# A hybrid decoder layer on one core: weight differences issued earlier, and seven products in place of eight in part of the last gate projection

## The reference, cut to what matters

```
hn = rms_norm(h, ffn_norm)
h  = h + (silu(hn @ w_gate) * (hn @ w_up)) @ w_down          # 2048 -> 5632 -> 2048
gate = sigmoid(rms_norm(h, ple_norm) @ w_ple_gate)           # 2048 -> 2048, "the last gate projection"
h  = h + gate * (p @ w_ple_proj)                             # 256 -> 2048
```

## Time and profile before

| what | value |
|---|---|
| median of three runs | 1309.48 us |
| the profiled execution's own time | 1309.3 us |
| its span, first to last instruction | 1307.6 us |
| TensorE busy | 1300.2 us, 99% of the span |
| VectorE busy | 1025.2 us, 78% |
| ScalarE busy | 705.4 us, 54% |
| mean granted TensorE clock | 0.999 |

### The profile page before, as it was taken

One profiled execution on the slowest core, in us unless ns is written; L12 is line 12 of the kernel. 1 busy time (PEld: TensorE's weight loads), 2 busy tenths in 40 slices (PEclk: granted clock), 3 DMA queues, 4 the chain that ended last, 5 costly groups with the idle time before them and its releaser, 6 DMA issues.

```text
span 1307.6 us, 18471 instructions
## 1 busy us (share of the span) xinstructions
PE 1300.2 (99%) x6595; PEld 1073.5 (82%) x6595; DVE 1025.2 (78%) x1381; ACT 705.4 (54%) x937; POOL 56.6 (4%) x71
## 2 busy tenths in 40 slices
PE   9999999999999999999999999999999999999998
PEld 7788888887888887888888888888888888888887
DVE  6578885788586668999988987679888997968554
ACT  6576444543455566655555654445555555555643
POOL 5003000221000000000000000000000000000000
PEclk9999999999999999999999999999999999999999
DMA  8555544455434555665566656565566556556563
GB/s 272 177 177 162 161 146 130 146 149 152 145 119 145 184 170 165 218 213 186 183 208 205 198 189 210 186 212 187 191 206 209 191 178 210 194 178 207 193 201 138
DMA packets 126205, 238.38 MB, mean 182 GB/s; under 512 B 9711, under 2 KB 10786, under 8 KB 126138
## 3 DMA queue, kind: packets, MB, share of 16 engines
q1 hardware_dynamic: 126106, 237.48, 56.9%
q10 hardware_dynamic: 32, 0.01, 0.0%
HBM read 235.36 MB, written 2.10 MB: 182 GB/s over the span
## 4 chain that ended last, share of the span: by engine, by line
PE 97%; DVE 2%; ACT 0%; issue 0%; POOL 0%; DVEq 0%; ACTq 0%; POOLq 0%
PE pair L635 16%; PE pair L637 16%; PE pair L636 16%; PE pair L916 11%; PE pair L917 11%; PE pair L918 11%; PE bg L916 2%; PE bg L917 2%; PE bg L918 2%; PE bg L756 2%; PE bg L826 2%; PE bg L911 1%; PE bg L693 1%; DVE w_lo L1504 1%; PE bg L807 0%; PE bg L668 0%
## 5 line engine op out<-in xcount | busy, mean ns | idle before, releaser
L1504 DVE TENSOR_TENSOR w_lo<-raw,w_hi 128x1024 fp32r<-128x1024 f32 x442 | 533.4, 1222 | 180.9 <-ACT w_hi L1107 179.0
L1107 ACT ACTIVATE w_hi<-raw 128x1024 fp32r<-128x1024 f32 x401 | 419.3, 1056 | 274.9 <-PE pair L637 148.6
L635 PE MATMUL pair<-w_hi,xT_hi 128*128 128x512 f32 x780 | 314.3, 403 | 0.3 <-DVE w_lo L1763 0.2
L637 PE MATMUL pair<-w_hi,xT_lo 128*128 128x512 f32 x780 | 304.8, 391 | 0.0
L636 PE MATMUL pair<-w_lo,xT_hi 128*128 128x512 f32 x780 | 304.2, 390 | 0.0
L637 PEld LDWEIGHTS pair<-w_hi,xT_lo 128*128 128x128 f32 x780 | 146.4, 188 | 31.5
L635 PEld LDWEIGHTS pair<-w_hi,xT_hi 128*128 128x128 f32 x780 | 146.5, 188 | 29.9 <-issue 0.9
L636 PEld LDWEIGHTS pair<-w_lo,xT_hi 128*128 128x128 f32 x780 | 146.8, 188 | 27.3
L1379 ACT ACTIVATE w_hi<-raw 128x1024 fp32r<-128x1024 f32 x41 | 43.6, 1063 | 134.6 <-DVE raw L1830 133.1
L916 PE MATMUL pair<-w_hi,actT_hi 128*128 128x512 f32 x296 | 115.9, 392 | 0.0
L918 PE MATMUL pair<-w_hi,actT_lo 128*128 128x512 f32 x296 | 115.3, 389 | 0.0
(11 more groups left out here) (351 smaller groups left out, 1882.8 us busy)
## 6 DMA issues: line engine op xcount, KB each, us to landing
raw<-in_w_in_dram SPq DMA_DIRECT2D x112, 512.0 KB, 3.7
raw<-in_w_gate_dram SPq DMA_DIRECT2D x88, 512.0 KB, 4.4
raw<-in_w_up_dram SPq DMA_DIRECT2D x88, 512.0 KB, 4.5
raw<-in_w_down_dram SPq DMA_DIRECT2D x88, 512.0 KB, 4.7
raw<-in_w_o_dram SPq DMA_DIRECT2D x32, 512.0 KB, 4.0
raw<-in_w_ple_gate_dram SPq DMA_DIRECT2D x32, 512.0 KB, 4.5
raw<-in_w_ple_proj_dram SPq DMA_DIRECT2D x4, 512.0 KB, 4.2
h<-in_x_dram SPq DMA_DIRECT2D x3, 512.0 KB, 8.1
```

Source lines behind the costliest of these rows:

```text
L635: mm(banks[t][:], hi[:, ts], wh, start=first, stop=False)
L637: m = mm(banks[t][:], lo[:, ts], wh, start=False, stop=last)
L1107: f(w_hi[j % RING][:], raw[j % RING][:], ACT.Copy).then_inc(hi_ready, 1)
L1504: v.tensor_tensor(w_lo[j % RING][:], raw[j % RING][:], w_hi[j % RING][:].bitcast(F32), ALU.subtract).then_inc(lo_ready, 1)
```

## The change

There are two edits.

1. **Differences of the first mixed pair.** The four DVE differences for F5 and F6 were issued in the turn of F3, just before the remainder of F6. Now they are issued in the turn of F1 (`EARLY = 1`), after the remainder of F4 and before the DVE part of step `hA` 6. Two small buffers of the `hA` steps move elsewhere, and the fetch of F9 now also waits for the remainder of F5.
2. **Seven products in the last gate projection.** Blocks 0 and 1 are computed together in 16 units (`PG_SEQ`): five units of block 0 (k pairs 0, 1, 2, 3, 7), then three mixed pairs (k pairs 4, 5, 6), each followed by one plain unit of block 1, and two more plain ones. So L5/L6, L8/L9 and L11/L12 are mixed. Blocks 2 and 3 stay as they were. `hB` 4, 5 and 6 now also make four differences of activations each; `hB` 4 stands in the turn of P1, `hB` 5 in that of P2, `hB` 6 and 7 still in that of P3. ACT copies P1 to P3 out ahead of these steps and no longer behind. The squares of the last block of `h` move from the end of the down projection to the turn of L1, the sum over them to the turn of L3. The sums of partial results come in the turn of L12 and of L15, and block 0 is finished in the turn of L13, block 1 in that of L17.

```diff
-            at[(U_DB + FF_B * 8 // KU + 3, U_DB + FF_B * 8 // KU + 5, U_PP - 2, U_PP + 3)[n]][g].append(("hB", 2 * n + g))
+            late = (U_PP + 1 + g, U_PP + 3)[n - 2] if n > 1 else 0
+            at[late or U_DB + FF_B * 8 // KU + 3 + 2 * n][g if n != 2 else 0].append(("hB", 2 * n + g))
+EARLY = 1
+PG_MIXED = (4, 5, 6)
+PG_PLAIN = [g for g in range(UPB) if g not in PG_MIXED]
+PG_SEQ = ([(0, g) for g in PG_PLAIN] + [(0, PG_MIXED[0]), (1, PG_MIXED[0]), (1, PG_PLAIN[0])]
+          + [(0, PG_MIXED[1]), (1, PG_MIXED[1]), (1, PG_PLAIN[1])]
+          + [(0, PG_MIXED[2]), (1, PG_MIXED[2])] + [(1, g) for g in PG_PLAIN[2:]])
# SyncE, first gate/up block
                             sp.wait_ge(t4_ready, ...)
+                            if seq is FIRST_SEQ:
+                                sp.wait_ge(lo_ready, u0 + j - (RING - 1))
# TensorE, a mixed pair of the last gate projection
+                    use(u)
+                    product(bg[0][:], xT_hi[:, k0, a0], xT_lo[:, k0, a0], gh[:, 0, :], gl[:, 0, :], first, last)
+                    product(pair[0][0][:], xT_hi[:, k1, a0], ..., gh[:, 1, :], gl[:, 1, :], False, last).then_inc(unit_used, 1)
+                    use(u + 1)
+                    product(bg[3][:], E_hi[:, q, 0, :], ..., uh[:, 0, :], ul[:, 0, :], first, last)
+                    product(pair[1][0][:], E_hi[:, q, 2, :], ..., uh[:, 1, :], ul[:, 1, :], first, False).then_inc(unit_used, 1)
+                    pe.wait_ge(t3_lo_ready, MIX_PG + q + 1)
+                    product(bg[2][:], E_hi[:, q, 3, :], ..., t_hi[:, 2, :], t_lo[:, 2, :], first, last)
+                    pe.wait_ge(t24_lo_ready, MIX_PG + q + 1)
+                    product(bg[1][:], E_hi[:, q, 1, :], ..., t_hi[:, 0, :], t_lo[:, 0, :], first, last)
+                    product(pair[0][1][:], xT_hi[:, k1, a1], ..., t_hi[:, 1, :], t_lo[:, 1, :], False, last).then_inc(t_used, 1)
# ACT, step hB 4, 5, 6 (after the two scaled copies into xg)
+                            f(xT_hi[:, 2 * b:2 * b + 2, :], xg[:], ACT.Copy).then_inc(x_hi, 2)
+                            act.wait_ge(form_ready, 4 * (c + 1))
+                            f(E_hi[:, q, :, :], F_raw[:], ACT.Copy).then_inc(form_rounded, 1)
# ACT, turns of P0 to L31
+                if side and g in PG_MIXED:
+                    split_mixed(u + LEAD, u + LEAD, MIX_PG + PG_MIXED.index(g) + 1, False)
+                elif u + LEAD < UNITS:
                     split(u + LEAD, u + LEAD)
+                if u < U_PG:
+                    pp_end(u - U_PP)
                 for k in range(2):
                     for s in AT[u][k]:
                         post(*s)
+                if u == U_PG + 1:
+                    res_squares(3)
+                if u == U_PG + PG_END:
+                    act.wait_ge(t_used, MIX_PG + len(PG_MIXED))
+                    f(act_s[1][:], bg[0][:], ACT.Copy).then_inc(p1_copied, 1)
+                    act.wait_ge(h_rstd, 4)
+                    for t in range(NT):
+                        act.wait_ge(gate_sum, 2 * (FF_A + FF_B) + t + 1)
+                        f(gate_s[t][:], gate_s[t][:], ACT.Sigmoid, scale=h_rs[1][:, t:t + 1]).then_inc(pair_free[0], 1)
# DVE
+            def split_mixed(u, j, n, first, between):
+                if not first:
+                    dve.wait_ge(lo_ready, u)
+                    differences(u, j, n)
                 split(u, j)
...
                         split(u, j + LEAD)
+                    if peeled and n0 == 0 and j == EARLY:
+                        differences(u0 + seq.index(("up", MIXED[0])), seq.index(("up", MIXED[0])), m0 + 1)
                     if peeled:
                         for k in range(2):
                             for s in AT[u0 + j][k]:
                                 post(*s)
...
+                if u == U_PG + 3:
+                    dve.wait_ge(h_sq, 16)
+                    v.reduce_sum(h_s[1][:], h_ss[1][:], AX_X).then_inc(h_sum, 1)
+                if u == U_PG + PG_END:
+                    dve.wait_ge(p1_copied, done + 4 + 1)
+                    v.tensor_tensor(v_s[:], bg[1][:], act_s[1][:], ALU.add).then_inc(v_ready, 1)
+                    ...            # five more sums of 128x512, two of them ready for the sigmoids
+                if u == U_PG + PG_END + 1:
+                    finish(0, gate_s, pair_free[0], 2 * (B_PG // 2))
+                if u == U_PG + 2 * UPB - 1:
+                    wait_block(dve, u)
+                    dve.wait_ge(pg_parts, 2)
+                    for t, part in ((0, v_s), (1, u_s)):
+                        v.tensor_tensor(act_s[t][:], pair[1][t][:], part[:], ALU.add).then_inc(pair_free[1], 1)
+                if u == U_PG + 2 * UPB + 1:
+                    finish(1, act_s, pg_sig, 0)
```

More of the change, by code:

```diff
@@ L283, in build @@
         t3_raw = sb("t3_raw", [P, CB], at=mix + 62 * KIB)
-        d_raw = sb("d_raw", [P, 2, P], at=mix + 62 * KIB)
-        h1_raw = sb("h1_raw", [P, 2, P], at=mix + 63 * KIB)
+        d_raw = sb("d_raw", [P, 2, P], at=mix + 52 * KIB)
+        h1_raw = sb("h1_raw", [P, 2, P], at=mix + 53 * KIB)
         xg = sb("xg", [P, 2, TOK], at=mix + 58 * KIB)
@@ L512, in _ @@
                 load(U_PP + b, b, w_pp, 0, b * CB)
-            with sp.Fori(0, 2) as i:
-                for j in range(2 * UPB):
-                    load(i * (2 * UPB) + (U_PG + j), j, w_pg, KU * (j % UPB), i * (2 * CB) + j // UPB * CB)
+            for j, (side, g) in enumerate(PG_SEQ):
+                if j >= RING and PG_SEQ[j - RING] in [(0, m) for m in PG_MIXED]:
+                    sp.wait_ge(t4_ready, MIX_PG + PG_MIXED.index(PG_SEQ[j - RING][1]) + 1)
+                    fetch(j, w_pg, KU * g, side * CB)
+                else:
+                    load(U_PG + j, j, w_pg, KU * g, side * CB)
+            for j in range(2 * UPB, 4 * UPB):
+                load(U_PG + j, j, w_pg, KU * (j % UPB), j // UPB * CB)
             for b in range(3):
@@ new lines, in _ @@
+            a0, a1 = slice(0, P), slice(P, TOK)
+            pe.wait_ge(pair_free[0], 2 * (B_PG // 2))
+            for j, (side, g) in enumerate(PG_SEQ):
+                u = U_PG + j
+                k0, k1 = KU * g, KU * g + 1
+                if not side:
+                    wait_read(pe, ("hB", g))
+                if g in PG_MIXED:
+                    if side:
+                        continue
+                    q = PG_MIXED.index(g)
+                    first, last = q == 0, q == len(PG_MIXED) - 1
+                    if first:
+                        pe.wait_ge(pair_free[1], 2 * ((B_PG + 1) // 2))
+                        for n in PG_MIXED:
+                            wait_read(pe, ("hB", n))
+                    gh, gl = w_hi[j % RING], w_lo[j % RING]
+                    uh, ul = w_hi[(j + 1) % RING], w_lo[(j + 1) % RING]
+                    use(u)
+                    product(bg[0][:], xT_hi[:, k0, a0], xT_lo[:, k0, a0], gh[:, 0, :], gl[:, 0, :], first, last)
+                    product(pair[0][0][:], xT_hi[:, k1, a0], xT_lo[:, k1, a0], gh[:, 1, :], gl[:, 1, :], False,
+                            last).then_inc(unit_used, 1)
+                    use(u + 1)
+                    product(bg[3][:], E_hi[:, q, 0, :], E_lo[:, q, 0, :], uh[:, 0, :], ul[:, 0, :], first, last)
+                    product(pair[1][0][:], E_hi[:, q, 2, :], E_lo[:, q, 2, :], uh[:, 1, :], ul[:, 1, :], first,
+                            False).then_inc(unit_used, 1)
+                    pe.wait_ge(t3_lo_ready, MIX_PG + q + 1)
+                    product(bg[2][:], E_hi[:, q, 3, :], E_lo[:, q, 3, :], t_hi[:, 2, :], t_lo[:, 2, :], first, last)
+                    pe.wait_ge(t24_lo_ready, MIX_PG + q + 1)
+                    product(bg[1][:], E_hi[:, q, 1, :], E_lo[:, q, 1, :], t_hi[:, 0, :], t_lo[:, 0, :], first, last)
+                    product(pair[0][1][:], xT_hi[:, k1, a1], xT_lo[:, k1, a1], t_hi[:, 1, :], t_lo[:, 1, :], False,
+                            last).then_inc(t_used, 1)
+                    continue
+                use(u)
+                for kk in range(KU):
+                    k = KU * g + kk
+                    wh, wl = w_hi[j % RING][:, kk, :], w_lo[j % RING][:, kk, :]
+                    end = side == 1 and j == len(PG_SEQ) - 1 and kk == KU - 1
+                    o = pair[side]
+                    product(o[0][:], xT_hi[:, k, a0], xT_lo[:, k, a0], wh, wl, not side and k == 0, end)
+                    last = product(o[1][:], xT_hi[:, k, a1], xT_lo[:, k, a1], wh, wl, k == 0, end)
+                    if kk == KU - 1:
+                        last.then_inc(unit_used, 1)
@@ L1072, in _ @@
+            straight(U_PG + 2 * UPB, B_PG + 2, 1, UPB, lambda b, k: (xT_hi[:, k, :], xT_lo[:, k, :]))
             last_pair = pair[(B_PG + 3) % 2]
@@ L1135, in post @@
                         act.wait_ge(x1_full, 1)
-                    if step == "hA" and b in MIXED:
-                        if b - 1 in MIXED:
+                    if b in {"hA": MIXED, "hB": PG_MIXED}.get(step, ()):
```

(41 more changed lines are left out.)

57 lines of the change are left out of this document (28 added, 29 removed).

## The result

The changed kernel takes 1312.03 us (median of 22 runs, 1311.26 to 1312.66), the kernel before in the same comparison 1309.96 us (22 runs, 1309.24 to 1310.57). The ratio is 1.0016, with an interval of 1.0010 to 1.0021: slower by 2.1 us. The forecast was 1312.2 us and +2.7. That 1312.2 is met to 0.2 us is luck in part: the effect came out 0.6 smaller than forecast, and the median before 0.5 higher (1309.96 in this comparison, 1309.48 in the three runs that the forecast started from).

What follows compares the result with a forecast made beforehand. TensorE was taken as the bound, busy 1300.2 of 1307.6 us. Edit 1 +0.59, matmuls -2.04 and waits with restarts +4.16 gave +2.71, or 1312.2 us, with a range from 1308.2 to 1314.5.

Steps and rivals of the forecast that it cites:

- units I had named: TensorE waits for `w_lo` before F9 and F12 in the first block, then some six between L3 and L19.
- The saving's size, 2.04: Last gate projection: three pairs save three matmuls each, 9 x 0.2267 = 2.04 us.
- 0.59: Edit 1, first gate/up block: `hA` 7, F9 and F12 all come 0.59 us later, and TensorE with them.
- the wait before F9, 1.35: First gate/up block: TensorE's first wait would be near 1.35 us and not 0.76.
- 2.12: Edit 2's net loss in us, from the terms -2.04 for matmuls and +4.16 for waits with restarts.
- The walk: Queues followed from P0: waits 0.90, 0.56, 0.53, 0.46, 0.56, 0.31, with six restarts 4.16 us together.
- the wait before L19: Last gate projection: block 1's sums and sigmoids make L19 0.31 us late.
- The 216 ns: The skill's warm matmul price for 512 columns, set beside the row's 0.2267 us; by it the saving would be 1.94.
- The terms that I put at nothing: GpSimd's power beside VectorE in the last projection put at 0; landings of 5.0 us taken as covered but around L16.
- adding up to 1.55: By the skill's rule on VectorE and GpSimd contending in SBUF, up to 1.55 us would be added; forecast put 0.
- 0.5 for slower: Chance 0.50 of slower: 39 of the forecast's 55 above 0.2% over the median (1312.1 us), with the late fetches.
- 0.41 for the band: Chance of same, within 0.2% (2.6 us): the fed pairs, the half waits and the other 16 of the forecast.

Runs made afterwards that it cites:

- e6: The changed kernel with the squares in the turn of P0, `hB` 4 in the last down unit but one, `hB` 5 behind P1's last product; ratio 0.9988.
- e3: The kernel before with the differences of F5/F6 in the turn of F1, behind step `hA` 6; ratio 0.9993.

## Why the prediction held, and where its sizes were off

**Direction and mechanism: right.** Seven marked waits, for `w_lo` from VectorE, at units I had named, and nine matmuls less. An eighth, of 0.10 before F7, I had not named, and I said L19 would wait; it does not. The saving's size, 2.04, is borne out by e6 (1.97).

**Edit 1: right in sign, 0.42 and not 0.59.** The step that was mis-sized is the start of the differences. I let them begin 0.09 after the remainder of F4 had ended, as in the turn of F3. There they wait for that remainder; here they don't, and they overlap its end. VectorE's timeline of the changed kernel, on a clock that runs 0.13 late at this place (bursts 502.46 and 502.33):

```profile
502.44 1.23 DVE L1586 TENSOR_TENSOR w_lo<-raw,w_hi 128x1024 fp32r<-128x1024 f32 x1 [1.20 <-ACT w_hi L1166]
503.59 0.69 DVE L1914 TENSOR_TENSOR t_raw<-raw 128x512 f32<-128x512 f32 x1
...
506.37 0.41 DVE L1637 TENSOR_TENSOR d_raw<-bg,h_raw 128x256 f32<-128x256 f32 x1
...
510.96 1.23 DVE L1586 TENSOR_TENSOR w_lo<-raw,w_hi 128x1024 fp32r<-128x1024 f32 x1 [1.24 <-ACT w_hi L1447]
```

`d_raw` is at 506.24 on the old clock (506.43 said, 504.18 before), F6's remainder at 510.83 (511.01 said), behind 1.24 of idle time for ACT (1.22 said). The chain is as walked. What TensorE makes of it is not quite: I had the whole shift in the wait before F9, 1.35. It is 0.96 there, as F7 is late already, by 0.10 and a restart.

**Edit 2: 1.55 and not 2.12.** Less the shift of 0.55 that F12 has gathered, L3 starts at 1224.82 (1224.81 said), L6 at 1232.18 (1232.31), L9 at 1240.29 (1240.46), L12 at 1248.34 (1248.54), L17 at 1263.53 (1263.52). The walk holds to 0.2. What failed is the wait before L19, 0.31 + 0.14: I made ACT's two sigmoids of block 1 wait for both sums of VectorE. The first waits for the first only. In the two timelines of the changed kernel the sums are at 1265.08 and 1265.68, the sigmoids start at 1265.79, and L19's remainder is there 0.6 sooner than I had it:

```profile
1265.08 0.68 DVE L2091 TENSOR_TENSOR act_s<-pair,v_s 128x512 f32<-128x512 f32 x1
1265.68 0.68 DVE L2091 TENSOR_TENSOR act_s<-pair,u_s 128x512 f32<-128x512 f32 x1
1268.11 2.36 DVE L1586 TENSOR_TENSOR w_lo<-raw,w_hi 128x1024 fp32r<-128x1024 f32 x2 [1.75 <-ACT w_hi L1166]
```
```profile
1265.79 1.34 ACT L1564 ACTIVATE act_s<-act_s,h_rs 128x512 f32<-128x512 f32 x2 [4.92 <-DVE act_s L2091]
```

Of the difference of 0.57 that is 0.45; the five waits, 2.94 where I had 3.01, make 0.07, and the remaining 0.05 is within the tenth to which the span is given. (The restarts behind these waits took 0.12 to 0.18, where I had 0.14.)

The price of a matmul came from the row and held: 9 x 0.2267 = 2.04 against e6's 1.97. The 216 ns that stand beside it in the prediction need a word more: the Trainium skill (TensorE: Matmul & The Clock Gate, Back-to-back issue gap) gives them for a single matmul by itself. For a stream of weight loads and matmuls, which this is, the same section has about 131 ns at 512 columns. The traces here don't bear that out: they have 226.7 ns.

**The terms that I put at nothing.** GpSimd's two operations run at 1234.57 to 1237.30 in the changed kernel, and the two remainders of VectorE beside them take 2.35, as elsewhere; a difference that starts at 1236.78, with the power still under way, takes 0.69, as elsewhere. The rule of the Trainium skill (SBUF — State Buffer, Who interferes with whom) by which one of two such operations is blocked shows on GpSimd alone: its power took 1554 ns here and 699 before, when VectorE was idle beside it but for the last 0.14 us. The rule has the later of the two blocked, and in both traces VectorE's remainder had started first (1234.40 against 1234.57; 524.10 against 524.27 before). So the trace did not speak against it, as I had put it, and adding up to 1.55 was no fair reading of it. One fetch in the pairs held up a rounding (L15's at 1251.79, 1.08 of ACT's idle time), while VectorE still had remainders to do from 1250.49 to 1254.1, so nothing came of it. Fetches held up four more from 1273.14 on; TensorE waited for none of these units.

**Rivals and chances.** I had put the edge of what a measurement tells at 0.2%, and the result of 0.16% is on the near side of it. With 22 runs of each kernel the interval, 0.10% to 0.21%, is still clear of no change: the edge was finer than I had it. My 0.5 for slower by over 0.2% against 0.41 for the band was a little heavy on the far side, because I took what a walk leaves out to add time; both slips of mine were waits that I had made too long. They went the same way and added up, to the 0.6 by which +2.7 was too much.

## What to carry to other kernels

A saving on the bounding engine comes through only if its feeders have lead where it is placed: nine matmuls were worth 1.97 us once ACT had 4 us of work moved to turns where it idled, and turned into a loss of 1.55 without. When an operation is moved sooner in an in-order queue, ask which step of another engine's it now stands in front of: ahead of `hA` 6 it cost 0.42, behind it, in the same turn, it gained 0.61. And a walk of the queues from the rows of the trace found the starts of the late units to 0.2 us; the one wait that it made up, before L19, came of two semaphores taken as one.

## What the runs showed of the hardware

The start of the kernel varies by about as much as edit 2 costs and over three times what edit 1 does: with the same instructions up to there, the burst in F1 came between 502.02 and 503.52 us in eleven executions. Distances between two marks inside the traces agreed to within 0.06 us between kernels that are alike in the stretch (28.62 to 28.68 in the six that have edit 1's order, 27.60 in both that have e3's).

A short wait costs more than itself: behind each of the five in the last projection, 15 matmuls took 3.52 to 3.58 us where 15 in a row take 3.40. GpSimd's small power took 699 ns with VectorE almost idle and 1554 ns beside VectorE's remainders in the changed kernel; these took as long as ever (2.35 us for two).
